# Mixing a head over two passes in layer 0, and the first output tiles in eight pieces

## The reference

```python
h = rms_norm(x, norm_g) * (1.0 + scale) + shift
qa, ka, va, ra, ga, qb, kb, vb, gb = split_cols(h @ w_in, EVEN_SIZES)
# heads 0..3: gated linear attention; heads 4..7: retention with rotary phase
oa, gla_s = chunked_recurrence(gla_chunk, gla_s0, (q, k, v, log_a), GLA_CHUNK)
oa = rms_norm(oa, gla_norm_g) * silu(ga)
ob, ret_s = chunked_recurrence(retention_chunk, ret_s0, (rotary(q), rotary(k), v), RET_CHUNK)
ob = rms_norm(ob, ret_norm_g) * silu(gb)
x + gate * (concatenate([oa, ob]) @ w_out)
```

## The kernel before

| behind unit | TensorE | VectorE, ScalarE |
|---|---|---|
| start | | clamp of the gate rows (L1454) |
| 2 | cumulative sums (heads 0 to 3) or the half swap of the rotation (4 to 7) | decays by Exp, or the rotation (L1464 to L1467); scaling (L1469, L1470); the gates' sigmoid, three Activates |
| 3 | transposes of values, small rows of the samples | gate product (L1473), copy of small rows (L1475), masked keys (L1477), token values |
| 7 | transposes of keys, scores | scores masked (L1481), token keys |
| 8, 9 | state products, four chunks each | four state steps each (L1493 to L1500); GpSimd scales the carries (L1939) |
| 12, 13 | samples' outer products (8 rows), outputs of one value half | samples' states (L1508), copy of the outputs |
| 16, 17 | samples' outputs, one column a matmul | |
| 21 | sum of squares over the features | copy (L1514), squares, addition (L1517) |
| 22 | | reciprocal root, norm and gate product into `wide` (L1521, L1522) |

## Time and profile before

### The profile page before, as it was taken

The page is one execution under the profiler, slowest core; times in us unless marked ns, Lnnn a source line. Parts: engine busy times, 40 slices in busy tenths (PEclk is TensorE's granted clock), DMA queues, the critical chain, the costliest instruction groups (busy, mean ns, idle before and its releaser), DMA issues.

```text
span 2440.2 us, 45909 instructions
## 1 busy us (share of the span) xinstructions
PE 2238.2 (92%) x17191; PEld 1977.7 (81%) x17191; DVE 1161.6 (48%) x3560; ACT 598.4 (25%) x741; POOL 192.3 (8%) x301
## 2 busy tenths in 40 slices
PE   6799999999998989689979987999999998999997
PEld 2189888888887978689968887888788787788997
DVE  1542333424243343434363256776677766755332
ACT  1322121212122121222232232232222222233221
POOL 0000101101010101000000001011011011000110
PEclk9899899989999899879989999999999999999999
DMA  9977454545645464223442245777878877854442
GB/s 317 315 218 214 141 173 155 150 147 160 192 148 164 133 182 155 71 73 110 119 143 75 73 122 200 261 254 257 268 244 270 274 239 240 267 181 130 135 130 61
DMA packets 400019, 437.02 MB, mean 179 GB/s; under 512 B 16916, under 2 KB 306990, under 8 KB 399167
## 3 DMA queue, kind: packets, MB, share of 16 engines
q1 hardware_dynamic: 359270, 311.99, 41.9%
q0 software_dynamic: 30752, 113.67, 13.4%
q10 hardware_dynamic: 9810, 8.73, 1.1%
HBM read 407.79 MB, written 26.54 MB: 178 GB/s over the span
## 4 chain that ended last, share of the span: by engine, by line
PE 66%; DVE 15%; DMA 8%; issue 5%; ACT 4%; POOLq 1%; POOL 0%; DVEq 0%; SPq 0%; ACTq 0%
PE pt L507 50%; PE m L507 14%; DMA arena<-in_cache_k 6%; DVE arena L1636 4%; ACT arena L916 2%; ACT w_hi L916 2%; DVE w_lo L1276 1%; DMA raw<-in_e_w_ada 1%; PE m L511 1%; DMA arena<-in_o_k_norm_g 1%; POOLq L1878 1%; DVE arena L1447 1%; PE pt L511 0%; DVE arena L1794 0%; DVE arena L1393 0%
## 5 line engine op out<-in xcount | busy, mean ns | idle before, releaser
L507 PE MATMUL pt<-act_hi,w_hi 128*128 128x260 f32 x4384 | 924.1, 293 | 63.6 <-DVE act_lo L1359 23.2
L507 PE MATMUL pt<-act_hi,w_lo 128*128 128x260 f32 x4384 | 897.0, 287 | 0.0
L507 PE MATMUL pt<-act_lo,w_hi 128*128 128x260 f32 x4384 | 896.7, 287 | 0.0
L507 PEld LDWEIGHTS pt<-act_hi,w_hi 128*128 128x128 f32 x4384 | 693.1, 194 | 126.5 <-issue 96.8
L1276 DVE TENSOR_TENSOR w_lo<-raw,w_hi 128x1024 fp32r<-128x1024 f32 x274 | 335.3, 1224 | 906.7 <-ACT w_hi L916 906.2
L507 PEld LDWEIGHTS pt<-act_lo,w_hi 128*128 128x128 f32 x4384 | 693.2, 193 | 0.0
L507 PEld LDWEIGHTS pt<-act_hi,w_lo 128*128 128x128 f32 x4384 | 691.0, 193 | 0.0
L916 ACT ACTIVATE w_hi<-raw 128x1024 fp32r<-128x1024 f32 x274 | 289.6, 1057 | 1170.3 <-PE pt L507 1155.0
L1636 DVE CUSTOM_DVE_ANT_0 arena<-arena 128x128 f32<-128x128 f32 x1024 | 224.9, 286 | 104.8 <-DMA arena<-in_cache_k 104.5
L916 ACT ACTIVATE arena<-arena 128x1040 f32<-128x1040 f32 (+8 forms) x199 | 169.7, 864 | 281.2 <-DVE arena L1730 81.7
L507 PE MATMUL m<-arena 128*128 128x128 f32 (+7 forms) x1136 | 210.0, 348 | 6.9 <-POOL arena L1939 4.1
(11 more groups left out here) (161 smaller groups left out, 1096.6 us busy)
## 6 DMA issues: line engine op xcount, KB each, us to landing
arena<-in_cache_k POOLq DMA_DIRECT2D x128, 512.0 KB, 4.9
arena<-in_cache_v SPq DMA_DIRECT2D x128, 512.0 KB, 5.1
raw<-in_o_w_in SPq DMA_DIRECT2D x112, 512.0 KB, 5.6
raw<-in_e_w_in SPq DMA_DIRECT2D x98, 512.0 KB, 4.4
raw<-in_e_w_ada SPq DMA_DIRECT2D x96, 512.0 KB, 5.7
raw<-in_o_w_ada SPq DMA_DIRECT2D x96, 512.0 KB, 5.4
raw<-in_e_w_out SPq DMA_DIRECT2D x32, 512.0 KB, 4.1
raw<-in_o_w_out SPq DMA_DIRECT2D x32, 512.0 KB, 4.8
```

Source lines behind the costliest of these rows:

```text
L507: return pe.matmul(out, lhsT, rhs, start=start, stop=stop, skip_group_check=True)
```

## The change

`mix0` is cut in two generators on TensorE, ScalarE and VectorE (GpSimd's stays). `first0(i)` holds everything up to the first half of the state; it runs in pass i itself, once the fourth tile is evacuated. `rest0(i)` holds the second half of the state and all behind it, and runs in pass i+1. `passed(rest, first)` joins them: nothing at the start, the rest's steps behind units 2, 3, 8, 9, 12, 13 and 16 (none behind 7), the first's behind 17, 21, 22, 23, 26 and 27.

| behind unit | TensorE | VectorE, ScalarE |
|---|---|---|
| 2 | state products, second four, of head i-1 | four state steps |
| 3, 8 | outer products and outputs | samples' states, copies; at 8 the gate clamp |
| 9 | samples' outputs, both halves | sigmoid, gate product |
| 12 | | copy, squares, addition |
| 13, 16 | sum of squares (13) | root (13), mixed rows (16) |
| 17, 21 | sums or swap of head i (21) | decays (21) |
| 22, 23 | transposes (23) | rotation, scaling (22); small rows, token values (23) |
| 26, 27 | key transposes, scores (26); state products, first four (27) | scores masked (26); four state steps (27) |

The gate clamp, sigmoid and product move from the first steps into `rest0`. In the output stretch only `rest0(7)` is left, and the four units are worked on in eight pieces around it. The last store counts on another semaphore. The core of the diff:

```diff
+        def passed(rest, first):
+
+            yield
+            for n in range(8):
+                if n != 2:
+                    go_on(rest)
+                yield
+            for n in range(6):
+                go_on(first)
+                yield
...
-            def mix0(i, gla):
-                yield
-                pe.wait_ge(s("evac"), i * 6 + (T_L0 + 6))
+            def first0(i, gla):
+                yield
+                pe.wait_ge(s("evac"), i * 6 + (T_L0 + 4))
+                if isinstance(i, int) and i == 0:
+                    pe.wait_ge(s("la_copied"), 2)
+                    pe.wait_ge(s("const_in"), 16 * NCONST)
+                else:
+                    pe.wait_ge(s("o_rs"), i)
...
+                key_values(i, 0)
+                yield
+
+            def key_values(i, half):
+
+                if half:
+                    pe.wait_ge(s("s_step"), i * 8 + 4)
+                else:
+                    pe.wait_ge(s("ktok"), i + 1)
+                for n in range(4 * half, 4 * half + 4):
...
+            def rest0(i):
+                key_values(i, 1)
                 yield
                 pe.wait_ge(s("s_step"), i * 8 + 8)
...
             with pe.Fori(1, HEADS) as i:
-                l0(i, mix0(i - 1, True))
-            l0(HEADS, mix0(HEADS - 1, True))
+                l0(i, passed(rest0(i - 1), first0(i, True)))
+            l0(HEADS, passed(rest0(HEADS - 1), first0(HEADS, False)))
             with pe.Fori(HEADS + 1, 2 * HEADS) as i:
-                l0(i, mix0(i - 1, False))
...
+            rest = rest0(2 * HEADS - 1)
+            go_on(rest)
+            for u, part, goes in ((0, (0, 4), True), (0, (4, 8), True), (1, (0, 4), True), (1, (4, 8), True),
+                                  (2, (0, 6), True), (3, (0, 6), True), (2, (6, 8), False), (3, (6, 8), False)):
+                t, hh = OUT_FIRST[u]
+                if hh == 0 and part[0] == 0:
                     pe.wait_ge(s("evac"), T_OUT0 + t - 1)
-                tile_unit("out0", 0, u, hh, (T_OUT0 + t) % 2, 1 if t == 0 else None, mix)
-            finish(mix)
+                tile_unit("out0", 0, u, hh, (T_OUT0 + t) % 2, 1 if t == 0 else None, part=part)
+                if goes:
+                    go_on(rest)
+                if u == 2 and part[0] == 0:
+                    go_on(rest)
+            finish(rest)
```

VectorE's part of the output stretch (ScalarE's is alike, with `hi` for `lo` and its last two splits behind `take(15)`):

```diff
+            rest = rest0(2 * HEADS - 1)
+            go_on(rest)
+            for c in range(8):
+                take(1, c)
+            go_on(rest)
+            take(1, 8)
+            take(1, 9)
+            lo("out0", 0, 2)
+            go_on(rest)
+            take(1, 10)
+            take(1, 11)
+            go_on(rest)
+            take(1, 12)
+            take(1, 13)
+            lo("out0", 0, 3)
+            finish(rest)
+            take(1, 14)
+            take(1, 15)
+            dve.wait_ge(s("act_ready"), 32)
+            evac_first(0, 2)
+            lo("out0", 0, 4)
+            evac_first(1, 3)
+            lo("out0", 0, 5)
```

More of the change, by code:

```diff
@@ L517, in unit_ready, with tile_unit @@
                 return tile_no(name, i if isinstance(i, int) else 0, u) % 2
-            def tile_unit(name, i, u, hh, par, stage, mix=None, turn_=None):
+            def tile_unit(name, i, u, hh, par, stage, mix=None, turn_=None, part=(0, 8)):
                 b = unit_ready(name, i, u)
                 turn_ = hh if turn_ is None else turn_
-                for k in range(8):
+                for k in range(*part):
                     c, at = 8 * hh + k, 8 * turn_ + k
@@ L533, in tile_unit @@
                         go_on(mix)
-                last.then_inc(s("pe_tile"), 1)
+                if part[1] == 8:
+                    last.then_inc(s("pe_tile"), 1)
                 go_on(mix)
@@ L1036, in mix0 @@
                     yield
+                act.wait_ge(s("g_clamp"), i + 1)
+                sigmoid(pair_c).then_inc(s("g_sig"), 1)
                 yield
@@ L1059, in _ @@
                 step.body(i, HEADS + 1, 3)
-                l0(i, mix0(i - 1, False))
+                l0(i, passed(rest0(i - 1), first0(i, False)))
             step.end(HEADS - 2, 3)
[L1062 to L1078, removed]
+            l0(2 * HEADS - 1, passed(rest0(2 * HEADS - 2), first0(2 * HEADS - 1, False)), ahead=(0, 1))
+            rest = rest0(2 * HEADS - 1)
+            go_on(rest)
+            act.wait_ge(s("pe_tile"), tile_no("out0", 0, 0))
+            for c in range(8):
+                take(c)
+            go_on(rest)
+            take(8)
+            take(9)
+            hi("out0", 0, 2)
+            go_on(rest)
+            take(10)
+            take(11)
+            go_on(rest)
+            take(12)
+            take(13)
+            hi("out0", 0, 3)
+            finish(rest)
+            act.wait_ge(s("mixed"), 16)
+            take(14)
+            take(15)
+            hi("out0", 0, 4)
+            hi("out0", 0, 5)
             for t in range(2):
@@ L1471, in mix0 @@
                 yield
-                dve.wait_ge(s("g_sig"), i + 1)
-                step(tt(g45, g45, pair_c, ALU.mult))
                 dve.wait_ge(s("v_t"), i + 1)
@@ L1484, in mix0, with state_steps @@
                 yield
-                for n in range(NCH):
+                state_steps(i, 0)
+                yield
+            def state_steps(i, half):
+                dve.wait_ge(s("kv"), i * 2 + (half + 1))
+                for n in range(4 * half, 4 * half + 4):
                     at = 6 * (n // 2) + n % 2
-                    if n % 4 == 0:
-                        if n:
-                            yield
-                        dve.wait_ge(s("kv"), i * 2 + (n // 4 + 1))
                     kv = M[n % 2][:, 128 * (n % 4 - n % 2):128 * (n % 4 - n % 2) + 256]
@@ L1586, in out0, with evac_first @@
                 finish(mix)
[L1588 to L1606 removed]
+            def evac_first(t, u):
+                dve.wait_ge(s("pe_tile"), tile_no("out0", 0, u) + 1)
+                evac_out0(0)(t, pt[(T_OUT0 + t) % 2][:, :, 0:HALF]).then_inc(s("evac"), 1)
+            rest = rest0(2 * HEADS - 1)
+            go_on(rest)
+            for c in range(8):
+                take(1, c)
+            go_on(rest)
+            take(1, 8)
+            take(1, 9)
+            lo("out0", 0, 2)
+            go_on(rest)
+            take(1, 10)
+            take(1, 11)
+            go_on(rest)
+            take(1, 12)
+            take(1, 13)
+            lo("out0", 0, 3)
+            finish(rest)
+            take(1, 14)
[5 more added lines that the diff above has]
+            lo("out0", 0, 5)
             add_squares(0, 0, True)
@@ L1998, in _ @@
             pool.wait_ge(s("ys"), 16)
[L1999 to L2000 removed]
+            pool.dma_start(a["y_sample_out"].rearrange("b o d -> (b o) d"), yrow).then_inc(s("y_out0"), 16)
+            for name, value in (("y_out0", 144), ("y_out1", 128), ("st_out", 128), ("s_out", 128), ("kv_out", 512),
                                 ("cv_out", 128)):
```

91 lines of the change are left out of this document (35 added, 56 removed).

## The result

The kernel after took **2426.25 us** in the median of 13 runs (2417.67 to 2437.63), the kernel before 2443.66 us in 13 runs on the same chip: a ratio of **0.9936 [0.991, 0.9962]**, 15.6 us less, where 19.6 were forecast. The executions that are profiled took 2419.26 us (span 2417.7) and 2441.72 us (span 2440.2), 22.5 us apart.

What follows compares the result with a forecast made beforehand. TensorE, busy 92% of the span, was taken to set the time. Passes +1.2 us, output stretch -24.8 and clock +4 summed to -19.6 us, giving 2419 us by the median, range 2400 to 2440.

Steps and rivals of the forecast that it cites:

- Part 1: Passes: waits for small rows (L1475) and sum of squares (L1517) go, 1.7 and 1.5 us per pass; "issue" waits stay.
- Parts 2 and 3: New waits: 1.3 us at unit 21 in all eight passes, 1.9 us at unit 23 in passes 4 to 7.
- Part 4: Rest of the passes: second state half hidden with 0.5 us margin, gates' sigmoid free, fourth modulation load taken as 0.
- Part 5: Sum of passes: pass 0 +6.8 us, passes 1 to 3 -6.0, pass 4 +0.4, passes 5 to 7 0.0; total +1.2.
- Part 6: Output stretch: 90.7 us before, TensorE goes on at 65.9, so -24.8; ends at 56 and 81 us by the clock.
- Part 7: Clock in passes: bounds -6 us (first outer products) and +12 (samples' outputs, modulation); taken +3, plus +1 at the end.
- (a): Rival: clock stays up in the output stretch and at the first halves, -39 us, 2400 us; chance 0.15.
- (b): Rival: clock stays down through the whole output stretch, -5 us, 2434 us, no change; chance 0.12.
- (c): Rival: state half at unit 2 or fourth modulation load is late, +7 to +14 us, about 2430 us; chance 0.08.
- (d): Rival: clock falls further at three places in each pass, +23 us, 2462 us; decides at some 36 us more; chance 0.08.
- (e): Rival: parts fail, as when a wait counted gone remains, 3 us a pass less gain, 2440 us; chance 0.03.

Runs made afterwards that it cites:

- e6: Kernel before with only the gates' clamp, sigmoid and product moved to units 13 and 16: 2439.99 us, ratio to before 0.9957.
- e2: Kernel after with VectorE evacuating the fourth tile ahead of its split at unit 17: 2422.16 us, ratio to before 0.9918.
- e3: Kernel after with VectorE's rotation and scaling moved from behind unit 22 to behind unit 21: 2413.45 us, ratio to before 0.9904.
- e1: Kernel after with the three small per_head loads counted on a semaphore other than the constants': 2420.33 us, ratio to before 0.9922.
- e9: Kernel after with e1, e3 and e4 together, without the early evacuation: 2406.65 us, ratio to before 0.9857.
- e5: Kernel after with unit 3 of the output stretch run whole after unit 2, instead of cut in two: 2432.74 us, ratio to before 0.9937.
- e4: Kernel after with GpSimd fetching x once both value tiles are copied, not after the last operand piece: 2424.23 us, ratio to before 0.9934.
- e7: Kernel after with the samples' outputs in two steps, behind units 9 and 12: 2426.24 us, ratio to before 0.9897.

## Why the prediction was right, and where not

**Direction and size held**: 2426.25 us measured, 2419 forecast. By the ratio the gain is 15.6 us, and 19.6 were forecast.

**Part 1, the old waits: right.** L1475 and L1517 are gone from every pass. e6 shows the cause of the first, which the forecast had not separated from the rest: 9.1 of its 12.1 us go with the gates alone. The part said that the "issue" waits stay; 10.8 us became 6.0. The two of the loop of gated-linear-attention heads (2.2 and 1.6 us) went; those of the retention loop went from 7.0 to 6.0. All twelve executions with the split mixing have 5.5 to 6.5 us of it. No run explains that; e6 rules out the gates.

**Parts 2 and 3, the new waits: right**, 8.6 us in 7 (9.1 forecast) and 7.9 in 4 (7.6). e2 and e3 take each away by moving what VectorE does ahead of them. In pass 0 the wait of 1.3 us shows only where the 10.8 us are gone and the evacuation is not early (e1, e9).

**Part 4: right.** No wait for a carry, a state step or a modulation load of over 0.2 us stands in the passes; the margin of 0.5 us held.

**Part 5, the sum of the passes: the step that failed.** It says "pass 0 gains the first part of head 0 ..., together 5.5, plus 1.3 = +6.8". The 5.5 is sound (4.4 of it ahead of the end of unit 27, and measured so in e1); the 1.3 was 10.8, and the low clock behind it cost 3.9 more. The step looked only at what the sums read, the evacuated tile. Their order in the program also holds the wait for the constants, and in the kernel before that wait stood ahead of the same sums at 233.6 us, when its last load had long landed. The timeline of before has what was needed to see it:

```profile
199.69 1.91 PE L507 MATMUL m<-raw,cond 128*9 128x512 f32 x16
...
202.09 0.69 DVE L1447 TENSOR_SCALAR arena<-pt 128x520 f32<-128x520 f32 x1
...
205.35 0.66 SPq L340 DMA_DIRECT2D per_head<-in_o_sb_offset  x1
...
206.54 1.28 SPq L340 DMA_DIRECT2D per_head<-in_o_b_s  x1
```

The modulation of unit 21 ends at 201.6 and the evacuation at 202.8, so the moved sums are wanted there; the last load is issued at 206.54 and, by the 5.8 us to landing, there at 212.3: a wait of some 10.7 us behind the modulation, as came. The seven other passes, forecast at -5.6 us, gave 9.8 more with the "issue" waits and the clock. Pass 0 missed by +16.0 (9.5 of wait, 3.9 of clock, 3.9 from before the first moved step, less the 1.1 of state products), they by -9.8, or -12.8 with the +3 of Part 7, the other two stretches by -3 each. That the total is near is luck: misses of both signs cancel, and the part of the clock in them is not the kernel's, for with e5's passes in after's place the span would have missed by +8.5.

**Part 6, the output stretch: right**, 62.8 us for 65.9. The pauses were forecast at 5 to 6 at the start and 4 at the end, and are 5.4, 5.1 and 3.7. The 3 us lie between the first operand pieces and the last pause, 46.2 us forecast, most of it at a clock of 0.74, and 42.3 measured at 0.83. e4 and e5 confirm what the step says of x: its transfer is uncovered and makes 2.0 of the last 3.7 us, and a whole unit there covers it.

**Part 7, the clock: not borne out, and not to be judged from one execution.** In after's profile the first outer products did become like the second. The seven stretches in after, for the earlier trace rows (42.59 us, mean 6.08), the last row their sum; passes 2 to 4 show the same duration and the same clock:

```profile
367.26:372.54 5.28, 5.28 (x34) 0.85 0.34 98
473.09:478.37 5.28, 5.28 (x35) 0.85 0.30 85
578.83:584.07 5.24, 5.24 (x35) 0.86 0.28 80
...
sum 35.75, PE 35.75; mean PE 5.11
```

That is -6.8 us where -6 stood in the bounds; in e5's execution of the same passes they come to 40.6 us, only some 2 us less than before. The +12 against it, for falls at the samples' outputs, did not come: they ran at the full clock in six passes of seven. New falls came instead, of 3.41 us each, behind the wait at unit 21 in passes 1 to 3. From unit 21 of pass 1 to that of pass 4 the clock falls three times a head at the same places: 2.0 to 2.2 us behind the start of the sums, and in either outer products of the next pass. e1 and e4 have the same three; e3, e5, e7 and e9 have the same waits and no fall there, so the wait alone does not bring it. The passes as a whole have 61 us at the low level, 68 before: -3.4 us, forecast +3; but e5 has 85, which would be +8.5, so the sign stays open. The Trainium skill ("TensorE: Matmul & The Clock Gate", Part 1) has the clock follow how busy the PE has been, and puts its practical advice as a bound on idle gaps. The trace agrees in pass 0, where the clock fell in a gap of 10.8 us and e1, without the gap, has none. Of the passes the bound says nothing, as it speaks of longer gaps than the 1.2 to 2.0 us there; the falls in them mostly have no gap ahead, like the one in the outer products at 367.3 us, which run at 0.85.

**Rivals.** (a) and (b) bounded the stretch from 56 to 81 us; it lies nearer to (a), at 62.8, but at a clock of 0.80. (c) is excluded by the waits. (d) did not come: the largest low-clock time of any execution with after's waits is 88.7 us (e7), 10 us of work over before, where (d) needed 36. (e) is out.

**What stays open**: why two "issue" waits went; what the cut of the samples' outputs is worth (21 us in one pair, 6 in the other) and through what; what places the falls of the clock, since the same instructions had 61 us of them in one execution and 85 in another; and so what the change itself does to the clock.

## What to carry to other kernels

When a step is moved earlier, list every wait that stands in front of it in its engine's order, and for each count on a semaphore every transfer that it sums, with its time of issue in the trace of before: a shared count makes a step wait for tables that it never reads. A stall that a move opens beside an engine with slack is often closed by swapping two instructions there (e3 took 9 us out of the passes by moving one `yield`). Measure such small parts in combination too: the early evacuation, within noise alone, was worth 13 us on top of three others, and the cut of the samples' outputs 21 us on top of it, though only some 6 on top of all four. And before a stage of two profiles is compared, take half of the low-clock time off each: the parts of this study then add up (12 for the change, 10 for the early evacuation, 9 for the rotation, 19 for both), where the bare times said that the early evacuation gained nothing.

## What the runs showed of the hardware that was not expected

- The granted clock falls at the same places pass after pass. In after, head 2 has falls at 429.0, 476.8 and 490.4 us, head 3 at 534.8, 582.6 and 596.2: each 105.8 us later, as its sums are. With the retention heads the pattern changes, and in e5, with the same passes, the falls lie elsewhere.
- Its sum is not fixed by the kernel: the same passes had 61.4 us at the low level in after's profile and 85.3 in e5's, 12 us of work apart, and 85.3 and 75.1 in the two executions of e2's kernel. That is more than most parts of this study are worth, and a single profile can't price the clock to better than that.
- Much of the spread of the runs has this size too: after's 13 runs have mean clocks from 0.942 to 0.950, which over 2426 us is 19 us of work, and times from 2417.67 to 2437.63.
- The three small loads into `per_head` took 5.5 to 6.0 us from issue to landing, as long as the 512 KB of modulation weights (5.4 us in the median).
